# Two blocks of a hybrid network on one core: the attention to the memory multiplies its values in split precision

## The reference

```python
def memory_cross_attention(h, mem, mem_g, wq, wk, wv, wo):
    bsz, seq, _ = h.shape
    m = rms_norm(mem, mem_g)
    q = (h @ wq).reshape(bsz, seq, XA_HEADS, XA_HEAD_DIM)
    k = (m @ wk).reshape(bsz, MEM_TOKENS, XA_HEADS, XA_HEAD_DIM)
    v = (m @ wv).reshape(bsz, MEM_TOKENS, XA_HEADS, XA_HEAD_DIM)
    s = jnp.einsum("bqhd,bkhd->bhqk", q.astype(jnp.float32), k.astype(jnp.float32)) * (XA_HEAD_DIM ** -0.5)
    pr = jax.nn.softmax(s, axis=-1)
    o = jnp.einsum("bhqk,bkhd->bqhd", pr.astype(v.dtype), v).reshape(bsz, seq, D_MODEL)
    return o @ wo
```

## Time and profile before

| | |
|---|---|
| median of 3 runs | 1662.91 us (1662.57 to 1663.62) |
| span of the profiled execution, from the first to the last instruction | 1663.1 us |
| the profiled execution's own time | not given apart from its span |
| busy, TensorE matmul | 1650.7 us |
| busy, TensorE weight load (overlaps the matmul) | 1328.3 us |
| busy, VectorE | 877.8 us |
| busy, ScalarE | 663.9 us |
| busy, GpSimd | 142.1 us |
| mean granted clock of TensorE, as a share of full speed | 0.999 |

### The profile page before, as it was taken

The page is one execution under the profiler, slowest core; times in us unless marked ns, Lnnn a source line. Parts: engine busy times, 40 slices in busy tenths (PEclk is TensorE's granted clock), DMA queues, the critical chain, the costliest instruction groups (busy, mean ns, idle before and its releaser), DMA issues.

```text
span 1663.1 us, 19085 instructions
## 1 busy us (share of the span) xinstructions
PE 1650.7 (99%) x7764; PEld 1328.3 (80%) x7764; DVE 877.8 (53%) x1161; ACT 663.9 (40%) x973; POOL 142.1 (9%) x162
## 2 busy tenths in 40 slices
PE   9999999999999999999999999999999999999999
PEld 7888878888878778888888878777767788888887
DVE  5446755555553454444443337766644677777321
ACT  5354334333553343332322335256584544444211
POOL 0000001211210010000000220311111100000000
PEclk9999999999999999999999999999999999999999
DMA  7222222232453122232333232332214223323331
GB/s 257 97 82 75 85 94 71 89 101 89 165 163 126 41 80 98 90 101 94 97 102 101 91 111 91 127 102 76 65 29 136 88 89 101 101 90 101 102 97 56
DMA packets 47462, 164.26 MB, mean 99 GB/s; under 512 B 5056, under 2 KB 5184, under 8 KB 47056
## 3 DMA queue, kind: packets, MB, share of 16 engines
q1 hardware_dynamic: 46192, 158.88, 29.5%
q0 software_dynamic: 896, 3.70, 0.7%
q10 hardware_dynamic: 288, 0.48, 0.1%
HBM read 158.81 MB, written 4.23 MB: 98 GB/s over the span
## 4 chain that ended last, share of the span: by engine, by line
PE 95%; DVE 2%; ACT 1%; issue 1%; DMA 0%; POOL 0%; SPq 0%; POOLq 0%; DVEq 0%; ACTq 0%
PE pst L414 94%; PE pst L579 1%; PE pst L862 1%; DVE XL L1620 1%; DMA raw<-wst 0%; ACT Sx L981 0%; ACT WH L981 0%; POOL acc L2325 0%; DVE WL L1608 0%; ACT L986 0%; DVE X L1825 0%; PE pst L703 0%; DVE ML L1616 0%; DVE qx L1840 0%; ACT XH L981 0%
## 5 line engine op out<-in xcount | busy, mean ns | idle before, releaser
L414 PE MATMUL pst<-XH,WH 128*128 128x512 f32 x1320 | 527.2, 399 | 0.6 <-DVE XL L1620 0.6
L414 PE MATMUL pst<-XH,WL 128*128 128x512 f32 x1320 | 514.4, 390 | 0.0
L414 PE MATMUL pst<-XL,WH 128*128 128x512 f32 x1320 | 514.1, 389 | 0.0
L1608 DVE TENSOR_TENSOR WL<-raw,WH 128x1024 fp32r<-128x1024 f32 x276 | 341.3, 1237 | 326.8 <-ACT WH L981 326.4
L981 ACT ACTIVATE WH<-raw 128x1024 fp32r<-128x1024 f32 (+1 forms) x278 | 291.1, 1049 | 337.5 <-PE pst L414 332.5
L414 PEld LDWEIGHTS pst<-XH,WH 128*128 128x128 f32 x1320 | 247.8, 188 | 63.8 <-issue 12.1
L414 PEld LDWEIGHTS pst<-XL,WH 128*128 128x128 f32 x1320 | 248.0, 188 | 52.9 <-issue 3.6
L414 PEld LDWEIGHTS pst<-XH,WL 128*128 128x128 f32 x1320 | 247.7, 188 | 52.1
L414 PE MATMUL pst<-HH,WH 128*128 128x512 f32 x352 | 136.9, 389 | 0.0
L414 PE MATMUL pst<-HL,WH 128*128 128x512 f32 x352 | 136.9, 389 | 0.0
L414 PE MATMUL pst<-HH,WL 128*128 128x512 f32 x352 | 136.9, 389 | 0.0
(11 more groups left out here) (255 smaller groups left out, 1783.0 us busy)
## 6 DMA issues: line engine op xcount, KB each, us to landing
raw<-wst SPq DMA_DIRECT2D x276, 512.0 KB, 3.5
X<-xT SPq DMA_DIRECT2D x7, 512.0 KB, 7.6
xs<-X SPq DMA_DIRECT2D x1, 2048.0 KB, 9.3
nC<-cd POOLq DMA_DIRECT2D x4, 512.0 KB, 5.2
X<-xs SPq DMA_DIRECT2D x2, 1024.0 KB, 5.6
outT<-X SPq DMA_DIRECT2D x8, 256.0 KB, 4.5
qx<-memT SPq DMA_DIRECT2D x1, 1024.0 KB, 4.8
gt<-cd POOLq DMA_DIRECT2D x1, 1024.0 KB, 8.9
```

The lines of the kernel that those rows point to most:

```text
L414: return nc.tensor.matmul(out, lhs, rhs, start=start, stop=stop)
L1608: vec.tensor_tensor(WL[:, i % NHL, :], raw[:, i % NRAW, :], WH[:, i % NHL, :].bitcast(F32), ALU.subtract).then_inc(wl, 1)
```

## The change

The values are kept as a high part vH and a low part vL, and so are the turned weights: PT[s] is now a pair of F32R buffers. ScalarE writes the high part of each (the copy that it made before, with F32R as its output), VectorE subtracts it from what stands in PSUM to get the low part. The products of values and turned weights go through `mm3`, three F32R passes each. TensorE's waits for ScalarE's copy before the second scores and before the products with the values become waits for VectorE's subtraction; those for the values become waits for vL. The subtraction of a half stands on VectorE in step 5, that of the other in step 9, as ScalarE's copies do. VectorE's count of a half goes from 5 to 6. The pairs of PT lie in MH and ML, and for head 2 in ZH and ZL; heads 0 and 3 share one, so ScalarE's copies for head 3 wait until head 0's products are done. Elsewhere two semaphores of the normalisations are dropped or merged into others (sqa and lns), which is not shown.

```diff
@@ -183,6 +183,7 @@
         raw = sb("raw", [P, NRAW, CH * P])
         WH = sb("WH", [P, NHL, CH * P], F32R)
         WL = sb("WL", [P, NHL, CH * P], F32R)
+        misc_at = nc.sbuf_base
         misc = sb("misc", [P, 6, T])
         acc = sb("acc", [P, 2, T])
         cm = sb("cm", [P, 5, P])
@@ -216,7 +217,8 @@
         st8 = sb("st8", [P, 16], stack=st)
         st.close()
         kx = sb("kx", [P, 8, MEM], stack=st)
-        vx = sb("vx", [P, 2, D], stack=st)
+        vH = sb("vH", [P, 2, D], F32R, st)
+        vL = nc.alloc_sbuf_tensor_at("vL", [P, 2, D], F32R, offset=misc_at + 4 * 2 * T)
         qx = sb("qx", [P, 8, T], stack=st)
         mrb = sb("mrb", [P, 4, MEM], stack=st)
         kT = qx[:, 4:8, :]
@@ -225,7 +227,8 @@
         ML = sb("ML", [P, 8, MEM], F32R, st)
         s8 = sb("s8", [P, 4, 8], stack=st)
         S2 = sb("S2", [P, 4, 2, MEM], stack=st)
-        PT = [misc[:, 4:6, :], misc[:, 2:4, :], acc[:, :, :], mrb[:, :, :].rearrange("p (a b) t -> p a (b t)", b=2)]
+        m_halves = [[w[:, a:a + 4, :].rearrange("p (a b) t -> p a (b t)", b=2) for w in (MH, ML)] for a in (0, 4)]
+        PT = [m_halves[0], m_halves[1], [ZH[:, 6:8, :], ZL[:, 6:8, :]], m_halves[0]]
         st.close()
         sty.close()
 
...
@@ -297,7 +300,7 @@
         x_add = sem("x_add")
         m_sq, m_ss, m_n, m_h = sem("mem_sq"), sem("mem_sumsq"), sem("mem_norm"), sem("mem_hi")
         m_l, kt_ok, kx_t, kx_ok = sem("mem_lo"), sem("kx_rows"), sem("kx_turned"), sem("kx")
-        qx_ok, vx_ok = sem("qx"), sem("vx")
+        qx_ok, vx_ok, vl_ok = sem("qx"), sem("vx"), sem("vx_lo")
         x_pe = [sem(f"cross_pe{s}") for s in range(4)]
         x_dve = [sem(f"cross_dve{s}") for s in range(4)]
         x_act = [sem(f"cross_act{s}") for s in range(4)]
@@ -668,7 +671,7 @@
                     if hf == 1:
                         keys(c)
                 for t in range(2):
-                    hold[(0, 1, 4, 5)[2 * hf + t]] = (vx_ok, 2 * hf + t + 1)
+                    hold[(0, 1, 4, 5)[2 * hf + t]] = (vl_ok, 2 * hf + t + 1)
 
             def queries():
                 for m in range(8):
@@ -695,7 +698,7 @@
                     hold[b0] = (x_act[s], 3 * i + 2)
                     yield
                     yield
-                    pe.wait_ge(x_dve[s], 5 * i + 5)
+                    pe.wait_ge(x_dve[s], 6 * i + 5)
                     free(b0)
                     for si in range(2):
                         for e in range(2):
@@ -703,14 +706,16 @@
                             ins = nc.tensor.transpose(ps[b0][:, o:o + P], S[:, e, si * P:(si + 1) * P], ident)
                     ins.then_inc(x_pe[s], 1)
                     yield
-                    hold[b0] = (x_act[s], 3 * i + 3)
-                pe.wait_ge(vx_ok, 2 * (s // 2) + 2)
+                    hold[b0] = (x_dve[s], 6 * i + 6)
+                pe.wait_ge(vl_ok, 2 * (s // 2) + 2)
+                th, tl = PT[s]
                 for dd in range(2):
                     b = b0 if dd == 0 else 3
                     free(b)
-                    pe.wait_ge(x_act[s], 6)
+                    pe.wait_ge(x_dve[s], 12)
                     for si in range(2):
-                        ins = mm(ps[b][:, :], vx[:, si, s * 256 + dd * P:s * 256 + (dd + 1) * P], PT[s][:, si, :], si == 0, si == 1)
+                        c = slice(s * 256 + dd * P, s * 256 + (dd + 1) * P)
+                        ins = mm3(ps[b][:, :], vH[:, si, c], vL[:, si, c], th[:, si, :], tl[:, si, :], si == 0, si == 1)
                     ins.then_inc(x_pe[s], 1)
                     yield
                 hold[b0] = (zl_ok, 8 + 2 * s + 1)
...
@@ -1217,7 +1222,7 @@
                     if c == 3:
                         act.wait_ge(mm_, DONE["wv_xa", 4 * hf + 3])
                         for t in range(2):
-                            run(ACT.Copy, vx[:, t, hf * 512:(hf + 1) * 512], ps[(0, 1, 4, 5)[2 * hf + t]][:, :]).then_inc(vx_ok, 1)
+                            run(ACT.Copy, vH[:, t, hf * 512:(hf + 1) * 512], ps[(0, 1, 4, 5)[2 * hf + t]][:, :]).then_inc(vx_ok, 1)
             turned(3)
 
             def queries():
@@ -1237,7 +1242,7 @@
                 for i in range(2):
                     yield
                     table(LNEXP)
-                    act.wait_ge(x_dve[s], 5 * i + 2)
+                    act.wait_ge(x_dve[s], 6 * i + 2)
                     if i:
                         act.wait_ge(x_pe[s], 2)
                     for e in range(2):
@@ -1246,7 +1251,9 @@
                     yield
                     yield
                     act.wait_ge(x_pe[s], 2 * i + 2)
-                    run(ACT.Copy, PT[s][:, :, i * 256:(i + 1) * 256], ps[b0][:, :].rearrange("p (a t) -> p a t", t=256)).then_inc(x_act[s], 1)
+                    if s == 3:
+                        act.wait_ge(x_pe[0], 6)
+                    run(ACT.Copy, PT[s][0][:, :, i * 256:(i + 1) * 256], ps[b0][:, :].rearrange("p (a t) -> p a t", t=256)).then_inc(x_act[s], 1)
                 yield
                 yield
                 act.wait_ge(mm_, DONE["w_out", 7])
...
@@ -1845,8 +1852,15 @@
 
             follow(out_order, {"main": project("w_out", 0, "xa", lambda m: (x_in[m // 2], 32)), "mem": memory()})
 
-            for _ in range(16):
+            for _ in range(8):
                 chunk()
+            for hf in range(2):
+                for c in range(4):
+                    chunk()
+                for t in range(2):
+                    dve.wait_ge(vx_ok, 2 * hf + t + 1)
+                    d = slice(hf * 512, (hf + 1) * 512)
+                    lo(vL[:, t, d], ps[(0, 1, 4, 5)[2 * hf + t]][:, :], vH[:, t, d]).then_inc(vl_ok, 1)
 
             def queries():
                 for m in range(8):
@@ -1870,16 +1884,19 @@
                     yield
                     dve.wait_ge(x_pe[s], 2 * i + 1)
                     vec.tensor_reduce(m_[:, 0:2], pv, AX.X, ALU.max).then_inc(x_dve[s], 1)
-                    dve.wait_ge(x_dve[s], 5 * i + 1)
+                    dve.wait_ge(x_dve[s], 6 * i + 1)
                     vec.tensor_scalar(m_[:, 0:2], m_[:, 0:2], -1.0, None, ALU.mult).then_inc(x_dve[s], 1)
                     yield
                     dve.wait_ge(x_act[s], 3 * i + 2)
                     vec.reciprocal(m_[:, 4:6], m_[:, 2:4]).then_inc(x_dve[s], 1)
-                    dve.wait_ge(x_dve[s], 5 * i + 3)
+                    dve.wait_ge(x_dve[s], 6 * i + 3)
                     for e in range(2):
                         vec.tensor_scalar(S[:, e, :], S[:, e, :], m_[:, 4 + e:5 + e], None, ALU.mult).then_inc(x_dve[s], 1)
                     yield
                     yield
+                    dve.wait_ge(x_act[s], 3 * i + 3)
+                    lo(PT[s][1][:, :, i * 256:(i + 1) * 256], ps[4 + s][:, :].rearrange("p (a t) -> p a t", t=256),
+                       PT[s][0][:, :, i * 256:(i + 1) * 256]).then_inc(x_dve[s], 1)
                 yield
                 yield
                 for dd in range(2):
```

More of the change, by code:

```diff
@@ L282, in program @@
         xh, xl = sem("xh"), sem("xl")
-        sqa, sqr, acp, ssq = sem("sq_acc"), sem("sq"), sem("acc"), sem("sumsq")
+        sqr, acp, ssq = sem("sq"), sem("acc"), sem("sumsq")
         rv, rl, rf, rdone = sem("mix_var"), sem("rms_ln"), sem("rms"), sem("rms2")
@@ L288, in program @@
         gz, u_ok, gu = sem("gelu_v"), sem("u"), sem("gelu_u")
-        lnd, lna, lns = sem("ln_dve"), sem("ln_act"), sem("ln_rsqrt")
+        lnd, lna = sem("ln_dve"), sem("ln_act")
         cv, cvh = sem("conv"), sem("conv_hi")
@@ L1002, in square @@
                 if k == 0:
-                    run(ACT.Square, acc[:, which, :], src, scale=scale).then_inc(sqa, 1)
+                    run(ACT.Square, acc[:, which, :], src, scale=scale)
                     return
@@ L1108, in norm_steps @@
                     act.wait_ge(lnd, 6)
-                    run(ACT.Ln, st8[:, 0:4], st8[:, 0:4]).then_inc(lns, 1)
-                    act.wait_ge(lns, 1)
-                    run(ACT.Exp, st8[:, 12:16], st8[:, 0:4], scale=-0.5).then_inc(lns, 1)
+                    run(ACT.Ln, st8[:, 0:4], st8[:, 0:4]).then_inc(lna, 1)
+                    act.wait_ge(lna, 5)
+                    run(ACT.Exp, st8[:, 12:16], st8[:, 0:4], scale=-0.5).then_inc(lna, 1)
                     yield
@@ L1731, in norm_steps @@
                     dve.wait_ge(row_in, 48)
-                    dve.wait_ge(lns, 2)
+                    dve.wait_ge(lna, 6)
                     for b in range(4):
```

## The result

The changed kernel takes 1666.33 us (median of 20 runs, 1664.57 to 1668.87) against 1663.59 (20 runs, 1661.47 to 1664.86): 2.74 us more, and as a ratio 1.0018, with a 95% interval of 1.0011 to 1.0024. The profiled execution has a span of 1665.8 us, 2.7 above that of before.

The account below looks back on a forecast made before the run. TensorE, busy 99% of the span, was taken as the bound. Waits of 5.81 us less a gain of 2.86 gave +2.95 on 1662.91, so 1665.9 us (0.18% slower), range 1664.2 to 1667.8.

Parts of the forecast that it names:

- The gain, 2.86 us: Products of values and turned weights on TensorE: 32 fp32 records at 0.43 us become 48 F32R passes at 0.227.
- The quarter that four passes would give, 3.44: Same products: the skill's rule of four passes for true FP32, three remaining, would gain 3.44 us; not taken.
- The subtractions for the values, nothing: Four VectorE subtractions for vL fit the gap before its next split and cost nothing.
- The price of a wait: Where TensorE waits for a late subtraction, it loses the subtraction's end + 0.16 us, less the start it had.
- The three large waits, 1.65 each: Subtraction behind an eviction: head 0's and 1's second scores, head 2's products with values; losses 1.65, 1.64, 1.65 us.
- The three small ones, 0.87: Head 2's second scores, head 3's second scores and products: subtraction slightly late, 0.29 us for head 3's scores, 0.87 in all.
- the two at nothing: Head 0's and head 1's products with the values: a head's scores, 1.7 us, and more stand ahead, so no loss.
- The rival of the clock: The clock falls at the new waits, adding 1.7 us per fall: 1667.6 with one, 1671 with three; chance 0.14.
- No large waits: Large waits do not come; 0 to 0.87 us lost, 2.86 gained: 1660.0 to 1660.9 us; chance 0.09.
- longer waits: Late subtractions delay VectorE's next work, or both upper bounds combine: +3.4 to +4.6 us, 1666.3 to 1667.5; chance 0.07.
- What could be told from no change: Whole kernel: a measurement can tell about 0.2%, 3.3 us, from no change; the forecast lay just inside it.
- A sign of being wrong: Wrong if, among other signs, any stage other than the attention's changed its length by over 0.5 us.

Follow-up runs that it names:

- gain_only: The change without the subtractions for the turned weights' low parts, TensorE and ScalarE waiting as before; stage 115.96 us against 118.78 before, ratio 0.9987.
- values_only: The kernel before plus the four values' subtractions on VectorE, results unused, banks and products waiting for them; stage 118.78 us, as before, ratio 1.0001.
- cost_only: The kernel before, fp32 products kept, plus the eight weight subtractions on VectorE, results unused, TensorE waiting for them; stage 124.65 us against 118.78, ratio 1.0038.
- dve_order_a: The change with one swap in VectorE's order, head 0's second-scores subtraction before the eviction m16; stage 120.19 us against the change's 121.86, one execution.
- best_order: The change with VectorE's swaps at m16 and m24 and the end of the stage reordered for all engines; stage 116.51 us, ratio to before 0.9989.
- wait_plus1: The change with one more unread subtraction on VectorE ahead of each of the three long-awaited ones; stage 125.21 us, one execution.

## Why the prediction was right

- **What bounds the kernel**: right. What TensorE gained and what it waited for went into the stage without loss, 5.87 - 2.82 = 3.05 against 3.08.
- **The gain, 2.86 us**: 2.82 by gain_only, and the difference is in the price of a pass. Inside a head's products the 39 distances from one F32R pass to the next in gain_only are 0.226 to 0.236 us, 0.229 on average; the term took 0.227, from a long stretch of such passes. With 0.229 it would be 13.76 - 11.01 = 2.75, and the last 0.07 was not followed up.
- **The quarter that four passes would give, 3.44**, is refuted as the gain. What fails in it is the price of what is left: it takes an F32R pass as a quarter of an fp32 product, 0.86 / 4 = 0.215 us, and the passes stand 0.229 apart. Three of them are 0.79 to 0.81 of an fp32 product by the distances 0.227 and 0.232, not 0.75. The Trainium skill, "FP8 and Floating Point Precision", TensorE Precision Notes, counts four passes for true FP32. The trace has two records for an fp32 product and can't tell how many passes lie in them, so it neither bears this out nor refutes it.
- **The subtractions for the values, nothing**: right, values_only, 0.00.
- **The price of a wait**, end of the subtraction + 0.16: right. Restart 0.06 behind its end and a first pass of 0.33, in the large and in the small ones; the next pass carries 0.10 of it at all six places.
- **The three large waits, 1.65 each**: right in place, number and size, 1.65, 1.66 and 1.65 in cost_only. dve_order_a gives 1.67 for the first. 1.4 us recorded at 536, 553 and 578 us, foreseen at 537, 553 and 579.
- **The three small ones, 0.87, and the two at nothing**: right, each shown by itself in cost_only: 0.28, 0.32 and 0.30, that is 0.90, and no delay added before head 0's and head 1's products. The same comparison of the change with gain_only, which share 529 matmuls, has the same six places and 5.9 us in all. With the swaps at the large ones, what is left over gain_only is 1.35 us: the three small ones, 0.9 there, and 0.44 before head 2's products.
- **The rival of the clock**: its mechanism is shown, its condition not met. At 1.4 us recorded, the clock was 1.00 in the stage behind all eight such waits in the profiled executions: three each in the change and in cost_only, two in dve_order_a. The margin is small: 0.6 us longer waits brought the first fall. That the total came out right hangs on this.
- **No large waits; longer waits**: both fell. The subtraction does stand behind the eviction, and nothing was late behind it.
- **The total**: 1665.9 predicted, 1666.33 measured. As a difference, 2.95 predicted and 2.74 measured (3.08 in the stage of the profiled executions); as a ratio, 1.0018 predicted and measured. The 0.4 us of the total come from the kernel before, which in 20 runs has a median of 1663.59 where 3 had 1662.91, less the 0.2 of the difference. In the terms two small misses add up: the gain was put 0.04 too high and the loss 0.06 too low.
- **What could be told from no change**: the prediction put it at 3.3 us. With 20 runs of either kernel the interval, 0.11% to 0.24%, excludes no change, though the 2.74 us lie below 3.3; that limit was too coarse.
- **A sign of being wrong**, another stage that changes its length by over 0.5 us: the program ahead of the stage was 0.77 us shorter in one execution, 0.64 of it within the first 13 us, long before anything that the change moves on TensorE. cost_only, with the program of before up to the stage, was 0.37 shorter there, so I don't put it down to the change.

## What to carry to other kernels

An engine that takes its queue in order makes a step wait for everything that stands in front of its producer, also for work of other streams. So when a wait moves from one engine to another, read what the new producer's engine does just before it, above all whether that in turn waits for the engine that will wait; here the fault was one of order, and swapping three pairs on VectorE gave back 4.5 of 5.9 us. Where TensorE has no idle time, a change of this kind is worth its passes only once every wait that it brings has a step of other work in front of it.

## What the runs showed of the hardware that was not expected

The fall of the clock at 1246 us, which I had read in the kernel before as a fixed part of it, comes in some executions and not in others, behind the same wait of 2.3 us. In the changed kernel and in values_only (window, busy by engine, granted clock):

```profile
1240.00:1258.00 18.00, 15.59 (x57) 10.77 (x56) 11.92 (x19) 13.03 (x20) 2.41 (x6) 0.91 0.44 167
```

```profile
1240.00:1258.00 18.00, 15.58 (x61) 10.48 (x61) 10.93 (x19) 11.89 (x20) 2.06 (x5) 1.00 0.51 176
```

Of the eleven profiled executions, those of before and of the change among them, nine have a fall between 1236 and 1262 us and two (values_only, best_order) have none. 18 us at 0.91 are 3.2 us at the lower level, half the full clock, and so 1.6 us of TensorE's time, which is about a tenth of a per cent of this kernel and over half of what the change moved. So single executions of it can't be compared by their span to better than that. In wait_plus1 the same was seen at three equal waits in one execution: two without a fall, before scores, and one with, before products with the values. So the recorded length of a wait alone doesn't decide. Whether the work around it does, or something that differs from one execution to the next, no run here tells.
